# Feed-forward up-projections with the weights' high parts over high and low inputs at once

## The reference, cut to what matters

```python
def causal_dwconv(x, w, b):          # three taps per channel in the feed-forward part
    ...
def conv_ffn(x, w_up, conv_w, conv_b, w_down):
    hid = causal_dwconv(x @ w_up, conv_w, conv_b)     # 1024 -> 2 * 2816
    gate, val = jnp.split(hid, 2, axis=-1)
    return (jax.nn.gelu(gate) * val) @ w_down         # 2816 -> 1024
...
x = x + rms_norm(conv_ffn(h, ffn_w_up[l], ffn_conv_w[l], ffn_conv_b[l], ffn_w_down[l]), g[3])
```

## Time and profile before

| | us |
|---|---|
| median of the runs | 1557.96 |
| profiled execution, its own time | 1559.52 |
| its span in the trace | 1557.8 |
| first feed-forward stage, about | 134 to 324 |
| second feed-forward stage, about | 470 to 685 |
| TensorE busy (matmuls) | 1519.2 |
| VectorE busy | 1052.8 |
| ScalarE busy | 835.1 |
| GpSimd busy | 191.4 |

### The profile page before, as it was taken

How to read it: one execution, slowest core, us unless ns; L and a number is a source line. 1 busy time by engine, 2 the same in 40 slices (tenths; PEclk the granted TensorE clock), 3 DMA queues, 4 the chain that set the end, 5 groups by cost and what they waited for, 6 DMA issues and landing times.

```text
span 1557.8 us, 23306 instructions
## 1 busy us (share of the span) xinstructions
PE 1519.2 (98%) x9044; PEld 1310.6 (84%) x9044; DVE 1052.8 (68%) x1928; ACT 835.1 (54%) x1518; POOL 191.4 (12%) x178
## 2 busy tenths in 40 slices
PE   7999999999999999999999999999999999999998
PEld 7988999979869888878888888787888888888887
DVE  6687777786768787876676566624646865555664
ACT  6876555565666656563323356634336264646564
POOL 0110121110000234311222000000003010000010
PEclk9999999999999999999999999999999999999999
DMA  7566666555346554652211211134222334333343
GB/s 264 163 236 222 222 216 215 189 201 193 112 160 221 188 169 159 204 172 96 84 66 55 81 55 52 44 95 133 97 95 96 121 116 130 119 121 117 102 137 121
DMA packets 64209, 219.54 MB, mean 141 GB/s; under 512 B 8154, under 2 KB 10458, under 8 KB 63972
## 3 DMA queue, kind: packets, MB, share of 16 engines
q1 hardware_dynamic: 60784, 214.27, 41.3%
q10 hardware_dynamic: 3316, 3.79, 0.8%
HBM read 216.93 MB, written 1.06 MB: 140 GB/s over the span
## 4 chain that ended last, share of the span: by engine, by line
PE 80%; DVE 11%; ACT 7%; issue 1%; DMA 1%; SPq 0%; DVEq 0%; ACTq 0%
PE PS L364 23%; PE PS L366 22%; PE PS L365 22%; DVE WL L331 4%; PE PS L2989 3%; ACT WH L314 2%; PE PS L535 1%; PE PS L2326 1%; PE PS L2303 1%; PE PS L2258 1%; PE PS L3019 1%; PE PS L2313 1%; ACT AR L1817 1%; DVE RH L559 1%; PE PS L877 1%
## 5 line engine op out<-in xcount | busy, mean ns | idle before, releaser
L331 DVE TENSOR_TENSOR WL<-RAWB,WH 128x1024 fp32r<-128x1024 f32 x345 | 435.8, 1266 | 215.2 <-ACT WH L314 209.4
L364 PE MATMUL PS<-RH,WH 128*128 128x256 f32 (+1 forms) x1560 | 497.7, 319 | 8.8 <-DVE RH L559 3.0
L366 PE MATMUL PS<-RH,WL 128*128 128x256 f32 (+1 forms) x1560 | 489.2, 314 | 0.0
L365 PE MATMUL PS<-RH,WH 128*128 128x256 f32 (+1 forms) x1560 | 489.2, 314 | 0.0
L314 ACT CAST WH<-RAWB 128x1024 fp32r<-128x1024 f32 x346 | 359.4, 1041 | 185.6 <-PE PS L366 173.8
L364 PEld LDWEIGHTS PS<-RH,WH 128*128 128x128 f32 x1560 | 297.2, 191 | 33.8 <-issue 5.9
L365 PEld LDWEIGHTS PS<-RH,WH 128*128 128x128 f32 x1560 | 297.4, 191 | 18.5 <-issue 0.7
L366 PEld LDWEIGHTS PS<-RH,WL 128*128 128x128 f32 x1560 | 297.2, 190 | 17.9
L364 PE MATMUL PS<-WH,RH 128*128 128x512 f32 (+1 forms) x768 | 302.8, 394 | 5.1 <-DVE WL L331 2.6
L365 PE MATMUL PS<-WL,RH 128*128 128x512 f32 (+1 forms) x768 | 296.0, 385 | 0.0
L366 PE MATMUL PS<-WH,RH 128*128 128x512 f32 (+1 forms) x768 | 295.9, 385 | 0.0
(11 more groups left out here) (384 smaller groups left out, 1597.0 us busy)
## 6 DMA issues: line engine op xcount, KB each, us to landing
RAWB<-ws SPq DMA_DIRECT2D x370, 512.0 KB, 3.5
AR<-ws SPq DMA_DIRECT2D x20, 512.0 KB, 4.7
X<-ws SPq DMA_DIRECT2D x4, 512.0 KB, 5.4
TMP<-gains SPq DMA_DIRECT2D x8, 256.0 KB, 4.9
AR<-stabilizers ACTq DMA_DIRECT2D x16, 128.0 KB, 3.1
CS<-cs SPq DMA_DIRECT2D x1, 1216.0 KB, 7.6
X<-x SPq DMA_DIRECT2D x2, 512.0 KB, 4.0
AR<-dec ACTq DMA_DIRECT2D x2, 512.0 KB, 7.0
```

Source lines behind the costliest of these rows:

```text
L331: eng.e.tensor_tensor(k.WL[:, i % SPL, :], k.RAWB[:, i % RAW, :], k.WH[:, i % SPL, :].bitcast(F32), ALU.subtract).then_inc(*eng.done("wl", i))
L364: pe.e.matmul(o, wh, xh, start=first, stop=False)
L365: pe.e.matmul(o, wh, xl, start=False, stop=False)
L366: return pe.e.matmul(o, wl, xh, start=False, stop=last)
```

## The change

A column block of the up-projections is computed by `project_wide`. The high and the low part of an input tile lie in one buffer, 2048 elements apart; a view (`L.wide`) takes both as one moving operand of 2 x 256 columns. One product of the weights' high part with this operand writes high by high into columns 0 to 255 of the bank and high by low into columns 256 to 511. A second product of 256 columns adds low weights by high input to the first half. The three sums are thus in two halves, which have to be added: ScalarE copies the second half into an SBUF buffer of a new ring of three (`UP`), VectorE adds the first half to it and frees the bank. The three taps then read this buffer, not PSUM. ScalarE's order in phase 0 becomes cast, copy, cast, copy, tap, tap, and VectorE's low part, sum, low part, sum, taps, taps. The low part of the hidden tile moves from VectorE to GpSimd, behind GpSimd's multiply of the step. The arena grows by 512 columns for two of the three buffers.

```diff
+def project_wide(k, pe, label, name, m, both, high, ready):
+    k.ws.begin(*label)
+    b = k.ps.take(pe, *label)
+    for n, i in enumerate(TURNS):
+        (wh, wl), end = weights(k, pe, True, name, i, m)
+        for sem, value in ready(i):
+            pe.wait_ge(sem, value)
+        pe.e.matmul(halves(b), wh, both(i), start=n == 0, stop=False)
+        mm = pe.e.matmul(b[:, 0:256], wl, high(i), start=False, stop=n == 7)
...
+        self.UP = k.ring(self.s + "up", [k.view(a, 256) for a in (12032, 13600, 13856)])
+        self.wide = k.RH[:, 8192:12288].rearrange("p (n i t) -> p i n t", n=2, i=8)
...
 ffn_pe
-               lambda i: (k.ACT.at(s, "yh", i), k.DVE.at(s, "yl", i)))
+               lambda i: (k.ACT.at(s, "yh", i), k.POOL.at(s, "yl", i)))
...
-            project(k, pe, (s, "up", m), f"ffn_up{l}", m, operand(L.HH), 256, ready)
+            project_wide(k, pe, (s, "up", m), f"ffn_up{l}", m, lambda i: L.wide[:, i], lambda i: L.HH[0][:, i, :], ready)
...
 ffn_act
             for m in (j, j + 22):
                 cast_to(k, act, k.ws.chunk(s, "up", m) + 2)
+                x = L.UP.take(act, s, m)
+                act.wait_ge(*k.PE.at(s, "up", m))
+                act_(x, k.ps.of(s, "up", m)[:, 256:512], ACT.Copy).then_inc(*act.done(s, "up", m, "low"))
+            for m in (j, j + 22):
                 g = L.GV.take(act, s, m)
-                act.wait_ge(*k.PE.at(s, "up", m))
-                act_(g, k.ps.of(s, "up", m)[:, 0:256], ACT.Identity, bias=k.P("fcb", l * 44 + m),
+                act.wait_ge(*k.DVE.at(s, "up", m, "sum"))
+                act_(g, L.UP.of(s, m), ACT.Identity, bias=k.P("fcb", l * 44 + m),
                      scale=k.P("fcw", (l * 3 + 2) * 44 + m)).then_inc(*act.done(s, "up", m))
...
 ffn_dve
             for m in (j, j + 22):
                 rest_to(k, dve, k.ws.chunk(s, "up", m) + 2)
-                g, b = L.GV.of(s, m), k.ps.of(s, "up", m)
+                x = L.UP.of(s, m)
+                dve.wait_ge(*k.ACT.at(s, "up", m, "low"))
+                v.tensor_tensor(x, k.ps.of(s, "up", m)[:, 0:256], x, ALU.add).then_inc(*dve.done(s, "up", m, "sum"))
+                k.ps.free(dve, s, "up", m)
+            for m in (j, j + 22):
+                g, b = L.GV.of(s, m), L.UP.of(s, m)
                 dve.wait_ge(*k.ACT.at(s, "up", m))
...
-                k.ps.free(dve, s, "up", m)
+                L.UP.free(dve, s, m)
...
         elif p == 2:
-            hi, lo = L.hid.of(s, j)
-            dve.wait_ge(*k.ACT.at(s, "yh", j))
-            v.tensor_tensor(lo, L.GV.of(s, j), hi.bitcast(F32), ALU.subtract).then_inc(*dve.done(s, "yl", j))
-            L.GV.free(dve, s, j)
...
 ffn_pool
+        else:
+            hi, lo = L.hid.of(s, j)
+            pool.wait_ge(*k.ACT.at(s, "yh", j))
+            pool.e.tensor_tensor(lo, L.GV.of(s, j), hi.bitcast(F32), ALU.subtract).then_inc(*pool.done(s, "yl", j))
+            L.GV.free(pool, s, j)
```

More of the change, by code:

```diff
@@ L18 @@
 TPC = 8
-NA = 13600
+NA = 14112
 NEG = -1e30
@@ L377, in project @@
         mm = three(pe, b, w, rhs(i), n == 0, n == 7)
+        if end is not None or n == 7:
+            mm.then_inc(*pe.done())
+        if end is not None:
+            pe.mark("weights", end)
+    pe.mark(*label)
+    k.ws.end(*label)
+def project_wide(k, pe, label, name, m, both, high, ready):
[7 more added lines that the diff above has]
+        mm = pe.e.matmul(b[:, 0:256], wl, high(i), start=False, stop=n == 7)
         if end is not None or n == 7:
```

## The result

The changed kernel takes 1591.02 us in the median of five runs (1587.77 to 1592.8) against 1558.5 us for the kernel before on the same chip: ratio 1.0207, 95% interval 1.0195 to 1.0218. It is 32.5 us slower, where +10.0 was forecast and the range ended at +19. The profiled execution took 1592.8 us with a span of 1590.6; its own time is 33.3 us over that of before.

What follows compares the result with a forecast made beforehand. TensorE was taken to bound both stages, with VectorE close behind in the second. -8.8 + 2.5 + 2.2 + 2.7 + 3.6 + 4.2 + 3.6 = +10.0 us on a median of 1557.96 gave 1568.0, range 1552 to 1577.

Steps and rivals of the forecast that it cites:

- The product's term: Both stages, 704 weight tiles: one 512- and one 256-column product replace three of 256, saving 8.8 us (0 to 9.2).
- The plain steps of stage 0: First feed-forward stage, ordinary steps: the longer chain fits under TensorE with half a us left, so they cost nothing.
- Step 1: End of stage 0: low part of hid 19, now on GpSimd, comes later and TensorE goes on 2.5 us later.
- end of stage 1: Second item: hid 20, 21 and the last low-part pass come late, costing 2.2 us (1.0 to 2.5).
- start of stage 1: Third item: VectorE's sums and taps delay what follows by 1.9 us, and 0.8 saved is lost: 2.7 (0.8 to 3.5).
- Step 4: Two filter steps with four 512-wide VectorE passes: the VectorE, ScalarE, VectorE loop outgrows TensorE's step, 3.6 us stall (0 to 6).
- Step 5: Two pairs of reciprocal steps in stage 1: VectorE's held low part and ScalarE's cast cost 4.2 us (0 to 8).
- Step 6: Context rows and filter together in stage 1: added sums and GpSimd turns delay the low part, 3.6 us (0.5 to 6).
- A: Filter and context stretches have more slack, only ends and start cost: -1.4 us, 1556.6; chance 0.19.
- B: GpSimd's instructions fall beside VectorE's PSUM reads, ends and start cost less: -5.7 us, 1552.3; chance 0.15.
- D: Wide product doesn't gain (strided operand, or the page's 2.5 ns), stalls shrink by half of it: +14 us, 1572; chance 0.07.
- C: VectorE bounds stage 1 as a whole, upper bounds hold in its later stretches: +18.6 us, 1576.6; chance 0.09.

Runs made afterwards that it cites:

- e8: Kernel after, with the 512-column product issued as two of 256 columns with the same weights: 1591.14 us.
- e7: Kernel after, but VectorE writes the sum into PSUM and all taps read PSUM: 1587.00 us.
- e16: Kernel after, with the low part of the hidden tile for tiles 6, 7, 15, 16 of stage 1 on VectorE: 1584.84 us.
- e5: Kernel after, with ten idle 256-column products ahead of nine down-projections at which TensorE waited: 1587.30 us.
- e14: Kernel before, plus VectorE's added sums and ScalarE's added copies with their results unused: 1570.54 us.
- e1: Kernel after, but the low part of the hidden tile stays on VectorE: 1574.92 us.
- e4: The whole change in stage 0 alone, stage 1 as in the kernel before: 1558.00 us.

## Why the prediction was right and wrong

**Right.** The sign, for the stated reason in kind: waits in stage 1 outweigh what the products save.

**The product's term was too large**, 8.8 us where the trace gives 5.6. Two column blocks of the kernel after, first two products of an unbroken run of 32, and the product behind it:

```profile
286.81 0.39 PE L394 MATMUL PS<-RH,WH 128*128 128x512 f32 x1
287.04 0.28 PE L395 MATMUL PS<-RH,WL 128*128 128x256 f32 x1
...
292.45 0.40 PE L364 MATMUL PS<-WH,RH 128*128 128x512 f32 x1
```

16 tiles in 5.64 us are 0.352 us a tile, against 0.360 in the earlier trace rows and in e8. In the whole trace, over 661 tiles at full clock, the step behind the 512-column product is 0.235 us on average, where I had 0.227 or 0.228, and the one behind the 256-column product 0.117, where I had 0.120. So a product less gave 8 ns, two thirds of the 12 to 13 that I had taken, and 704 tiles give 5.6 us. Whether the 7 ns come from the operand in two runs or from the alternation of the two widths is not shown. By the Trainium skill's warm gap for a single isolated product (TensorE: Matmul & The Clock Gate, Back-to-back issue gap) 2.5 ns would have been saved; for a stream of weight loads and products the page says that both set the spacing, so this rule is not for such a stream, and the 13 to 15 ns over N/2.4 in the earlier trace rows decide. The plain steps of stage 0 hold: no wait of 0.25 us or more in them.

**Durations.** What single instructions take in the kernel after (ns least/median/greatest):

```profile
L1566 ACT ACTIVATE AR<-PS x88: 369/383/387, 137.7 to 703.6; 128x256 f32<-128x256 f32 x88
L1570 ACT ACTIVATE AR<-AR,PR x88: 589/600/604, 140.8 to 704.5; 128x256 f32<-128x256 f32 x88
L1645 DVE TENSOR_TENSOR AR<-PS,AR x88: 407/417/426, 138.8 to 704.0; 128x256 f32<-128x256 f32 x88
L1651 DVE SCALAR_TENSOR_TENSOR AR<-AR,PR x176: 467/484/1189, 141.5 to 706.1; 128x255 f32<-128x255 f32 x88, 128x254 f32<-128x254 f32 x88
L1703 POOL TENSOR_TENSOR RH<-AR,RH x44: 730/1710/1733, 155.6 to 710.3; 128x256 fp32r<-128x256 f32 x44
```

Copy and sum as estimated (0.38, 0.42); the tap from SBUF takes 0.60 where I had 0.41. The sum, with one operand in PSUM, is never over 0.426, while the taps with both in SBUF now reach 1.19, where those of the earlier trace rows ended at 0.486. The Trainium skill (SBUF — State Buffer, Who interferes with whom) says that outside its two-port modes a VectorE instruction contends with GpSimd's reads only when it has two SBUF inputs; these rows and e7's longest tap of 0.485 agree.

**Step 1, end of stage 0** (+2.5): the wait came in the forecast order of engines, released by GpSimd's low part:

```profile
312.30 0.72 POOL L1698 TENSOR_TENSOR AR<-AR 128x256 f32<-128x256 f32 x1 [5.96 <-ACT AR L1588]
...
312.47 1.63 DVE L331 TENSOR_TENSOR WL<-RAWB,WH 128x1024 fp32r<-128x1024 f32 x1
312.99 1.70 POOL L1703 TENSOR_TENSOR RH<-AR,RH 128x256 fp32r<-128x256 f32 x1
...
314.83 0.77 PE L364 MATMUL PS<-WH,RH 128*128 128x512 f32 x1 [2.70 <-POOL RH L1703]
```

By starts 2.86 against 1.07 us before, so +1.8, and 3.0 for the clock behind it, which I had not counted.

**Steps 2, 3 and 4** were sized well as waits, by starts: end of stage 1 +2.1 (2.2), start of stage 1 3.43 against 0.64, +2.8 (2.7), the filter steps +4.2 (3.6). Step 4 is right in size but not in its releaser, so it is luck in part: its waits of 1.44, 1.65 and 1.81 us end with GpSimd's low part (twice) and GpSimd's filter sum (L2142), none with VectorE's low part of the weights, which the loop that I had worked through would give.

**Step 5 failed**, the pairs of reciprocal steps: "2.1 a pair, 4.2 in all" (its own four terms less the 1.05 make 2.2 a pair). The waits grew from 2.1 us to 13.6, by 11.5. I had worked the pair through for VectorE's held low-part pass and ScalarE's cast; what TensorE waited for was the hidden tile's own low part, queued on GpSimd behind a multiply that itself takes 3.21 to 3.46 us, no longer 2.46, and behind L2151 of 2.06. At the first wait of each pair the multiply is longer because VectorE, rid of the subtraction, begins its 1024-column pass 0.16 us ahead of it (559.18 above), and VectorE's next pass is held in turn (3.05); in the earlier trace rows and in e16 the pass begins 0.11 behind it and is the one held. I had priced the added instruction on GpSimd by its own duration and its turns, never by what stands before it in its queue. e16 shows the releaser and gives 6.2 us back with four tiles. What it leaves, 6.9 us of waits against 2.1 before, is +4.8: close to the 4.2, which had priced VectorE and ScalarE alone. The other 6.7 come from the low part's place on GpSimd.

**Step 6** had the right places and half the size: 7.6 us of waits against 1.3, +6.2 (3.6), again mostly for L1703, behind the context rows' subtractions on GpSimd: here 3.37 us for two.

```profile
620.76 3.37 POOL L597 TENSOR_TENSOR RH<-RB,RH 128x256 fp32r<-128x256 f32 x2
...
624.10 0.90 POOL L1698 TENSOR_TENSOR AR<-AR 128x256 f32<-128x256 f32 x1
...
624.97 0.91 POOL L1703 TENSOR_TENSOR RH<-AR,RH 128x256 fp32r<-128x256 f32 x1
626.02 0.77 PE L364 MATMUL PS<-WH,RH 128*128 128x512 f32 x1 [2.59 <-POOL RH L1703]
```

**Left out altogether: the clock.** Every wait was priced by its length, as if TensorE went on at 2.4 GHz; the sum has no term for it, and 11.8 us went there. In the trace's bookkeeping it is the largest miss, ahead of step 5 (+7.3), the product (+3.2) and step 6 (+2.6). The half clock follows from the waits, though, and e5 shows that removing more than half of it gives back less than it cost.

Put together for stage 1: waits +26.8 (forecast 16.3 of waits in steps 2 to 6), half clock +8.8 (0), product -2.8 (-4.4): +32.8 of +32.9 measured. For stage 0: waits +1.8, half clock +3.0, product -2.8: +2.0 of +1.7.

**The rivals.** A and B are excluded. D is excluded as a whole, since the product gains 5.6 us, but a third of the gain that I took is missing. C had the right picture, VectorE short of room in stage 1 (e14, with VectorE's and ScalarE's work alone, loses 12.5 us there), but at 1576.6 it was still 14 short, as it had neither the queue nor the clock.

**Open.** How the chain of e1 divides between waiting for a younger result and its other parts. Against e14 the chain with its products costs 4.4 us over the whole program and 7.3 in stage 1; 3.9 of the 7.3 is half clock (5.5 against 1.6). Nor is it known what sets which stretch goes to half clock: at the end of stage 0 the kernel after, e4 and e8 all wait 2.86 us, and 6.8, 3.4 and 0 us at half clock follow.

## What to carry to other kernels

Price an instruction that moves to another engine by where it lands in that engine's order: everything issued ahead of it, at the durations it will have beside the new neighbour. A saving per product counts only where TensorE sets the pace, and a wait of about 3 us cost about 1.6 to 3.0 us more where TensorE came back at 1.2 GHz, and nothing more where it did not. A change that lengthens the chain of four engines can be tried first in the stage where those engines have room, with its last steps left as they were.

## What the runs showed of the hardware

A kernel whose TensorE is busy 96% of the span still had 27 us at 1.2 GHz, each stretch in the two stages behind waits of 1.7 to 3.4 us, while the waits of 3.73 and 3.66 us had none behind them. Which of GpSimd's multiply and VectorE's 1024-column pass begins 0.1 us earlier decides which is held: the multiply takes 2.45 and the pass 3.41 us (e16), or the multiply 3.21 and the pass 1.16 (kernel after), and there the next pass takes 3.05. A product of 512 columns whose moving operand lies in two runs of 256, in alternation with products of 256 columns (0.117 us), took 0.235 us; among its own kind, with the operand in one run, it takes 0.228. An activation of 256 columns with scale and bias takes 0.60 us from SBUF and 0.56 from PSUM, so moving its input to SBUF gains nothing.
